# Sparse attention in a hybrid encoder layer: the leading keys' weights turned once per tile of queries and multiplied by zero-padded blocks of values

## The reference

```python
def dsa_attend(q, iq, iw, q_chunk, k, v, ik, k_chunk, n_sel):
    iscore = jnp.einsum('bqhd,bkd->bqhk', iq, ik).astype(jnp.float32) * IDX_SCALE
    score = jnp.einsum('bqhk,bqh->bqk', jax.nn.relu(iscore), iw.astype(jnp.float32)) * IDX_W_SCALE
    admissible = k_chunk[None, :] <= q_chunk[:, None]
    score = jnp.where(admissible[None], score, -jnp.inf)
    _, sel = lax.top_k(score, n_sel)
    ...
    logits = jnp.einsum('bqhgd,bqkhd->bqhgk', qg, k_sel).astype(jnp.float32) * ATTN_SCALE
    logits = jnp.where(sel_ok[:, :, None, None, :], logits, -jnp.inf)
    p = jax.nn.softmax(logits, axis=-1).astype(v.dtype)
    out = jnp.einsum('bqhgk,bqkhd->bqhgd', p, v_sel)
```

## Time and profile before

| | |
|---|---|
| median of three runs | 834.0 us |
| time of the profiled execution | 835.87 us |
| its span in the profile | 834.1 us |
| TensorE matmul busy | 794.2 us, 95% |
| VectorE, ScalarE, GpSimd busy | 328.4, 233.6, 181.2 us |
| mean granted TensorE clock | 0.992 |
| sparse attention stage | about 328 to 473 us |

### The profile page before, as it was taken

How to read it: one execution, slowest core, us unless ns; L and a number is a source line. 1 busy time by engine, 2 the same in 40 slices (tenths; PEclk the granted TensorE clock), 3 DMA queues, 4 the chain that set the end, 5 groups by cost and what they waited for, 6 DMA issues and landing times. The chain is left out here.

```text
span 834.1 us, 11845 instructions
## 1 busy us (share of the span) xinstructions
PE 794.2 (95%) x4611; PEld 490.9 (59%) x4611; DVE 328.4 (39%) x933; ACT 233.6 (28%) x476; POOL 181.2 (22%) x202
## 2 busy tenths in 40 slices
PE   7989999999999999999999998999899999999775
PEld 4465344588777667666666784555655555555542
DVE  5212564999154654544632265444611111111001
ACT  3021233111234454343333432121222222222111
POOL 2324440000042442000000001011133333333322
PEclk9999999999999999999999999999999999999998
DMA  8723120223300202004050299437899999999993
GB/s 269 205 102 110 27 91 11 84 74 134 122 2 1 102 1 84 26 2 151 1 102 1 81 409 404 133 122 269 272 390 397 400 398 400 396 396 394 405 398 107
DMA packets 59624, 155.80 MB, mean 187 GB/s; under 512 B 15464, under 2 KB 22088, under 8 KB 52400
## 3 DMA queue, kind: packets, MB, share of 16 engines
q1 hardware_dynamic: 50912, 141.75, 45.6%
q0 software_dynamic: 8656, 13.28, 6.0%
HBM read 147.38 MB, written 15.99 MB: 196 GB/s over the span
## 5 line engine op out<-in xcount | busy, mean ns | idle before, releaser
L856 PE MATMUL quad<-ring_w,xnT 128*128 128x512 f32 (+1 forms) x192 | 79.4, 554 | 0.0
L1907 POOL TENSOR_TENSOR arena<-arena 128x511 f32<-128x511 f32 (+5 forms) x36 | 35.6, 1008 | 155.1 <-DVE arena L2164 131.6
L1058 PE MATMUL pair<-xnT,ring_w 128*128 128x272 f32 x256 | 67.4, 402 | 0.4 <-ACT tabs L1646 0.4
L1174 PE MATMUL pair<-xnT,ring_w 128*128 128x272 f32 x256 | 65.8, 403 | 0.0
L1957 POOL DMA_INDIRECT out_y_prompt<-ring_w,idx x32 | 50.7, 1585 | 66.7 <-ACT ring_w L1813 66.1
L856 PE MATMUL quad<-xnT,ring_w 128*128 128x280 f32 (+1 forms) x256 | 60.6, 396 | 0.0
L1174 PEld LDWEIGHTS pair<-xnT,ring_w 128*128 128x128 f32 x256 | 46.5, 189 | 14.7 <-issue 6.0
L1058 PEld LDWEIGHTS pair<-xnT,ring_w 128*128 128x128 f32 x256 | 45.5, 190 | 15.8 <-issue 7.1
L856 PEld LDWEIGHTS quad<-xnT,ring_w 128*128 128x128 f32 x256 | 48.2, 190 | 10.8 <-issue 0.4
L1952 POOL DMA_INDIRECT ring_w<-xn_d,idx x32 | 33.1, 1036 | 93.9 <-PE quad L1420 45.1
L856 PEld LDWEIGHTS quad<-ring_w,xnT 128*128 128x128 f32 x192 | 34.3, 189 | 31.8 <-issue 26.0
(11 more groups left out here) (290 smaller groups left out, 1185.1 us busy)
## 6 DMA issues: line engine op xcount, KB each, us to landing
arena<-in_w_gate SPq DMA_DIRECT2D x21, 1024.0 KB
arena<-in_w_up SPq DMA_DIRECT2D x21, 1024.0 KB
arena<-in_w_down SPq DMA_DIRECT2D x40, 512.0 KB
ring_w<-in_w_in SPq DMA_DIRECT2D x8, 2048.0 KB, 8.4
ring_w<-in_w_down SPq DMA_DIRECT2D x20, 512.0 KB
xnT<-in_w_gate SPq DMA_DIRECT2D x4, 1024.0 KB
xnT<-in_w_up SPq DMA_DIRECT2D x4, 1024.0 KB
ring_w<-in_w_in SPq DMA_DIRECT2D x3, 1024.0 KB, 7.2
```

Of the source, the lines that this page charges most:

```text
L856: last = nc.tensor.matmul(o, l, r, start=i == 0, stop=i == len(mms) - 1)
L1058: last = nc.tensor.matmul(bank[6 + job % 2][:, 0:hi - lo], chunk8(6 + cb // 4)[:, k, c0:c0 + P], xT[:, k, lo:hi], start=k == 0, stop=k == ...
L1174: last = nc.tensor.matmul(bank[6 + job % 2][:, 0:hi - lo], w[:, k, c0:c0 + P], rhs[:, k, lo:hi], start=k == 0, stop=k == kt - 1)
L1907: nc.gpsimd.tensor_tensor(v, v, lb[:, i % LB, u, 1:n], ALU.mult).then_inc(w_ready, 1)
```

## The change

The leading keys are turned once per tile of queries. `pmeta` has room for 8 heads x 16 keys, 128 columns; the four jobs of a tile fill it, and after the last one a single transpose of 128 x 128 puts them into bank 3, 16 partitions per head. One copy of ScalarE takes them to `pTx`. `dvM` becomes eight blocks of 128 rows x 64 columns, one per query head: block `h` has the meta rows' values of its key/value head in rows 16h to 16h+15 and zeros elsewhere. So each head is a product of its own over all 128 rows. `dvM` moves into memory that the stick-breaking stage uses for its values, so GpSimd clears it after that stage's last sum and fills it with eight transfers; the wait of TensorE moves into `weigh_values`. The sample's job stays as it was.

```diff
@@ buffers
-        dvM = side[:, N_ROWS:N_ROWS + 2 * P].rearrange("p (u c) -> p u c", u=2)
-        pmeta = side[:, N_ROWS + 2 * P:].rearrange("p (i u c) -> p i u c", i=2, u=2)
+        pmeta = side[:, N_ROWS:N_ROWS + 2 * P].rearrange("p (i h c) -> p i h c", i=2, h=NH)
...
         pTx = carve(NH * P).rearrange("p (i c) -> p i c", i=NH)
+        dvM = carve(NH * HD).rearrange("p (h c) -> p h c", h=NH)
@@ SyncE
-            sp.wait_ge(dvm_zero, 1)
-            for u in range(2):
-                p0 = DEC + N_META * u
-                sp.dma_start(dvM[p0:p0 + N_META, u, :], dvP[DEC:DEC + N_META, NT - 1, :]).then_inc(dvm_in, 16)
@@ TensorE, before the sparse stage
-            pe.wait_ge(dvm_in, 32)
@@ TensorE, weigh_values
-                    ou = bank[3].rearrange("p (b u q) -> p b u q", b=2, u=2)
-                    for u in range(2):
+                    pe.wait_ge(dvm_in, 16 * NH)
+                    for g in range(4):
                         for kv in range(2):
-                            last = nc.tensor.matmul(ou[64 * kv:64 * (kv + 1), :, u, :],
-                                                    dvM[DEC:2 * DEC, u, 64 * kv:64 * kv + 64],
-                                                    pTx[DEC:2 * DEC, 2 * kv:2 * kv + 2, :],
+                            last = nc.tensor.matmul(o[64 * kv:64 * (kv + 1), g, :], dvM[:, 4 * kv + g, :], pTx[:, 2, :],
                                                     start=False, stop=True, skip_group_check=True)
@@ TensorE, after the transposes of a job
                     if t < NT - 1:
-                        last = nc.tensor.matmul(bank[3][DEC:2 * DEC, 0:P], pmeta[:, m % 2].rearrange("p u c -> p (u c)"),
-                                                ident, start=True, stop=True)
+                        if ends_tile(m):
+                            last = nc.tensor.transpose(bank[3][:, 0:P], pmeta[:, t % 2].rearrange("p h c -> p (h c)"), ident)
@@ ScalarE
-                    if t < NT - 1:
-                        x, xb = pTx[DEC:2 * DEC, b, :], bank[3][DEC:2 * DEC, 0:P]
...
+                    elif ends_tile(m):
+                        ins = nc.scalar.activation(pTx[:, 2, :], bank[3][:, 0:P], ACT.Copy)
+                    ins.then_inc(pT_copied, 1)
@@ GpSimd, at the start
-            link(nc.gpsimd.memset(dvM[DEC:2 * DEC], 0.0))
-            nc.gpsimd.sem_inc(dvm_zero, 1)
@@ GpSimd, after the stick-breaking stage
+            pool.wait_ge(pv_done, sums_done(NSB))
+            link(nc.gpsimd.memset(dvM, 0.0))
+            for h in range(NH):
+                kv = h // 4
+                pool.dma_start(dvM[N_META * h:N_META * (h + 1), h, :], dvP[DEC:DEC + N_META, NT - 1, 64 * kv:64 * kv + 64])\
+                    .then_inc(dvm_in, 16)
             pool.dma_start(wr[:, :, 0:4], a["w_group"].rearrange("(k p) c -> p k c", p=P)).then_inc(wr_in, 16)
@@ VectorE
-                    link(nc.vector.tensor_tensor(pmeta[:, m % 2], x,
+                    link(nc.vector.tensor_tensor(pmeta[:, t % 2, 2 * DSA_JOBS[m][1]:2 * DSA_JOBS[m][1] + 2], x,
```

More of the change, by code:

```diff
@@ L306, in build @@
         pTx = carve(NH * P).rearrange("p (i c) -> p i c", i=NH)
+        dvM = carve(NH * HD).rearrange("p (h c) -> p h c", h=NH)
+        assert at[0] <= 8896
         Lrow = arena[:, 0:DR * 2 * 544].rearrange("p (i c) -> p i c", i=DR)
@@ L462, in build @@
         iwp_in = sem("iwp_in")
-        dvm_zero = sem("dvm_zero")
         dvm_in = sem("dvm_in")
@@ L1735, in _ @@
                     act.wait_ge(pT_ready, m + 1)
-                    nc.scalar.activation(pTb[:, 2 * b:2 * b + 2, 0:n],
-                                         pairs[2].rearrange("p (u c) -> p u c", u=2)[:, :, 0:n], ACT.Copy)
-                    if t < NT - 1:
-                        x, xb = pTx[DEC:2 * DEC, b, :], bank[3][DEC:2 * DEC, 0:P]
-                    else:
-                        x, xb = pTx[0:DEC, 0:2, :], bank[3][0:DEC, 0:2 * P].rearrange("p (u c) -> p u c", u=2)
-                    nc.scalar.activation(x, xb, ACT.Copy).then_inc(pT_copied, 1)
+                    ins = nc.scalar.activation(pTb[:, 2 * b:2 * b + 2, 0:n],
+                                               pairs[2].rearrange("p (u c) -> p u c", u=2)[:, :, 0:n], ACT.Copy)
+                    if t == NT - 1:
+                        ins = nc.scalar.activation(pTx[0:DEC, 0:2, :],
+                                                   bank[3][0:DEC, 0:2 * P].rearrange("p (u c) -> p u c", u=2), ACT.Copy)
+                    elif ends_tile(m):
+                        ins = nc.scalar.activation(pTx[:, 2, :], bank[3][:, 0:P], ACT.Copy)
+                    ins.then_inc(pT_copied, 1)
             branches_copied(32)
```

## The result

The changed kernel takes 825.31 us (median of 4 runs, 823.23 to 826.29) against 834.31 us before: ratio 0.9888, 95% interval 0.9873 to 0.9902. Two more measurements, each beside the kernel before on the same chip, gave 824.26 against 834.2 (0.9881, 0.9858 to 0.9905) and 825.86 against 833.51 (0.9903, 0.9885 to 0.9920). The change makes the kernel about 1.1% faster, 9 us. The forecast was 827.3, with a range from 825.8 to 831.0: right in direction, too small in size.

A forecast was written before the change was run, and what follows sets the result against it. TensorE's instruction order was taken to bound the sparse stage, its gain reaching the end. Terms -6.5 + 0.4 - 0.6 = -6.7 us from the 834.0 us median gave 827.3 us, range 825.8 to 831.0.

The forecast's parts named there:

- What bounds the kernel: Sparse attention stage, 328 to 473 us: TensorE's instruction order sets the time, busy 9.99 of 10 us in a window.
- Rival C: End of program: weight stream's saturated part doesn't move, so the gain is lost (834) or halved (830.6); chance 0.07.
- Turning the leading keys, removed: Sparse stage, line 1281: 16 narrow turns gone, each 0.34 us plus 0.07 for the shape switch, saving 6.5 us.
- One turn per tile, added: Sparse stage, behind line 1277's transposes: four 128 x 128 transposes of the same shape, 0.11 us each, adding 0.44 us.
- Weighing: Sparse stage, lines 1195 and 1201: 16 instructions a tile without a shape switch between, gaining 4 x 0.15 = 0.6 us.
- Case B: Weighing in the sparse stage: the narrow products cost more, with times up to 831.0 us; chance 0.15.
- ScalarE, VectorE, GpSimd, SyncE: Other engines' work: 12 ScalarE copies fewer, GpSimd's added memset and eight transfers covered; each costed at nothing.
- a DMA queue at rest: Stretch where GpSimd's eight value transfers run: an idle DMA queue, taken as speaking against the values landing late.
- Rival D: First weighing, line 1201's place at 380 us: TensorE waits for late values, time up to 854 us; chance 0.03.
- A: Whole kernel: the sum of the terms holds, 827.3 us, from 826.2 to 829.1 with spread; chance 0.74.

## Why the prediction was too small

*What bounds the kernel:* right. TensorE's own order sets the stage, and a gain in it reaches the end whole: 8.6 us in the stage, 7.7 to 9.9 in the medians. Rival C, the gain spent in the weight stream, is refuted: SyncE issues the first weights of the experts at 465.67 us in place of 474.58, and the last weight transfer of the chain that ended last lands at 796.07, 797.40 and 799.23 us in the three profiles of the changed kernel, against 807.72 and 806.87 before. The run with the late values and that with narrow turns put back show the other sign of the same: 5.7 and 6.4 us more in the stage, and a time behind it of 359.5 and 358.3, within the spread.

*Turning the leading keys, removed:* the step that failed, "Removed: 16 x (0.34 + 0.07) = 6.5 us". It was the term that was mis-sized: a narrow turn costs 0.53 to 0.54 us, 16 of them 8.6. Two pieces were missed. The part ahead was read in the job of eight transposes as 0.97 against 0.93 of the stick-breaking stage and so averaged to 0.07. It is 0.10 there too (0.97 to 0.87). The yardstick of 0.93 wasn't clean, and the trace of the kernel before shows it. The eight stick-breaking transposes at 311.67 stand right behind the sums of line 1123, which are 64 columns wide. The next six stand behind products of full shape and hold TensorE 0.65 us, 0.11 each, which makes 0.87 for eight; the 0.06 more of the eight fits a switch of shape of their own:

```profile
314.60 0.82 PE L1100 MATMUL pair<-cst,arena 128*128 128x128 f32 x6
315.25 3.37 PE L1058 MATMUL pair<-xnT,ring_w 128*128 128x272 f32 x14
```

And I stopped counting at the start of the product behind the turn. Its first row has the full shape again, and 0.10 us more was hidden in that group: 1.57 us for six instructions where other such groups have 1.47. Going from start to start of single groups, I took the group behind for clean.

Time is lost on both sides of the turn: 0.10 ahead, and 0.34 - 0.22 + 0.10 = 0.2 behind, with the 0.22 of the second narrow turn. I had counted most of the first and half of the second.

*One turn per tile, added:* 4 x 0.11, as forecast.

*Weighing:* the total came out: a tile with two blocks takes 2.74 us against 2.88, a gain of 4 x 0.14 = 0.6 us. No run shows the 0.15 a tile of the forecast as such; it was my estimate. What the runs showed is made up as follows. The blocks of a tile are 16, 12, 8 or 4 instructions of 512 columns. To the start of the next group they take 3.58, 2.72, 1.87 and 1.01 us before (from 376.25, 410.24, 440.85 and 468.45) and 3.49, 2.63, 1.77 and 0.91 in the changed kernel (from 373.91, 405.74, 434.21 and 459.67). Four more take 0.85 to 0.86 us in both, 0.215 each, and beyond that 0.15 stands before and 0.05 after, so that 0.10 was the switch. The narrow products take 0.97, line 1201 took 1.01. At the rate of the 512 columns, 16 instructions of 128 would need 16 x 0.215 / 4 = 0.86, an estimate, so that 0.11 lies beyond the columns. Case B of the chances, that narrow products cost more, up to the 831.0 of the range, is refuted: 16 instructions take 0.97 us (435.98 to 436.95), 0.061 each, with their weight loads. These last 0.137 us each, 2.2 in sum, and all 16 lie between 435.55 and 436.78, so they overlap one another and the products.

*ScalarE, VectorE, GpSimd, SyncE:* nothing each, as forecast. The memset took 0.53 us, the eight issues 4.19; the residual rows still wait for TensorE, 34.7 us. The prediction took a DMA queue at rest for a sign against D; the DMA engines moved 401 GB/s from 330 to 334 us in the changed kernel. Even so the values landed by about 336.6, and TensorE needs them at 377.40. Rival D doesn't happen with 41 us of cover; with the values moved to the last moment the wait costs 5.7 us.

New sum by measured terms: -8.6 + 0.4 - 0.6 = -8.8 us, against 8.6 in the stage. With that term right, the forecast would have been 825.2 to 825.4. The chances had a slip of their own: A, B and half of C make 0.925, not 0.91.

## What to carry to other kernels

Where TensorE was busy for 9.99 of 10 us, the small odd-shaped product between products of full shape cost its switches, 0.3 us beside 0.22 us of work; turning 128 columns of which 32 are wanted, in the shape that the neighbours have, was cheaper than turning 32 (0.11 us against 0.53). Before merging many such products into one, change only their shape: that gave 6.8 of the 8.6 us with one line and a wider buffer (1.8 of them because a transpose is one instruction and the product two). When costing a removed instruction, compare the group before it and the group after it with clean groups of the same kind, not only the distance between starts.

## What was not expected of the hardware

Small transfers within SBUF landed 1.8 us after issue when SyncE issued them (kernel before), and 4.5 to 5.2 us after when GpSimd issued eight of them; SyncE's went at a DMA share of 0.04, GpSimd's for the most part at about 1, and no run parts the engine, the number and the load. A wait of 3.9 us of TensorE cost 1.7 us more afterwards, at a granted clock of 0.57 over the next 4 us. Rows of zeros cost nothing that shows: 16 products 128 deep took 0.97 us, 16 of the same columns 32 deep and with a switch behind them 1.02.
